# Dense expert gates: GpSimd scatter-adds into a cleared DRAM table instead of one-hot products on TensorE

## The chip, the cores and the metric

The kernel runs on one core of one Trainium2 chip. The metric is the device time of that core in microseconds, the median of several runs. All stages of two transformer blocks are one program, and one launch.

## The reference, cut to what matters

The kernel computes two blocks for 512 tokens of width 1024. The change lies in the last part of the first block, a layer of 16384 experts (128 x 128 keys), of which every token uses 8 x 16 = 128:

```
def peer_ffn(h, w_q, sub_keys, expert_u, expert_v):
    q = (ht @ w_q).reshape(T, 8, 2, 128)
    s = einsum('thpd,hpkd->thpk', q, sub_keys)
    top_s, top_i = top_k(s, 16)                  # per half
    cand = top_s[:, :, 0, :, None] + top_s[:, :, 1, None, :]
    best_s, best_c = top_k(cand.reshape(T, 8, 256), 16)
    expert_idx = ...                             # first key * 128 + second key
    gates = softmax(best_s)
    act = gelu(einsum('td,thkd->thk', x, expert_u[expert_idx]))
    return einsum('thk,thkd->td', gates * act, expert_v[expert_idx])
```

The kernel computes gelu(u_e . x) for all 16384 experts and all 512 tokens. For tokens 0 to 383 it multiplies them with a dense table of gates, which is zero where a token did not choose the expert, and takes the product with v as a dense matmul. The last 128 tokens are treated otherwise: for each of their 128 choices the row of v is fetched and added with its weight.

## The kernel before, in words

**Tiles of weights.** All weights come as a stream of 494 tiles of 128 x 1024 floats (512 KB). SyncE issues `load` (L453) into four slots `w_raw`; a load waits until the tile four places ahead has been split (`split_done`). A tile is split in two fp32r parts, hi (a rounded copy) and lo (the rest). TensorE makes 24 matmuls of 128 x 512 from it (L691 to L693: hi x hi, hi x lo, lo x hi, for eight column blocks). GpSimd's `split` (L558 and L560) makes hi and lo into two buffers `w_hi`, `w_lo`; it waits for the load and for the matmuls of the tile two places back.

**The first layer of experts** (tiles of u) is 128 tiles, one per first key. TensorE sums into banks 0 and 1; ScalarE's `key_act` applies gelu (L1653) and writes the 128 x 512 result to the DRAM tensor `acts` (L1655). Ahead of it are the 16 tiles of `peer_q` and the score matmuls (L971), whose results ScalarE copies (L1642). Alongside the first layer, VectorE makes the choices of each block of 128 tokens: `choose_halves`, `choose`, `places`, `pick_keys`, `chosen_gates`.

**The dense gates before the change.** For tokens 0 to 383, keys and gates of a block are transposed on TensorE (`turn`). VectorE's `one_hots` builds, for four tokens at a time, one-hot rows of both keys (L2437, L2439); GpSimd's `gate_batch` (L574) multiplies one of them with the gate; TensorE's `gate_batches` (L991) makes the 128 x 128 gates of a token as a product of one-hots, in two parts of 128 columns each. ScalarE copies one part (L1664), VectorE adds the other into `gate_stage` (L2449), and ScalarE writes 64 tokens at a time, 4 MB, to the DRAM tensor `gates` (L1676). `LOT_TILES` says how many tiles of u stand between two steps of eight tokens: there are 48 steps of 8 matmuls.

**The second layer of experts** (tiles of v) is 128 tiles in 64 units of two keys. SyncE's `load_unit` loads `acts_in` (L500), `gates_in` (L501) and the two tiles (L508). VectorE multiplies acts with gates (L2507), ScalarE and VectorE split the product (L1696, L2514) and the tiles (L1691, L2520), TensorE makes 24 matmuls of 128 x 384 from a tile. Meanwhile GpSimd fetches, with indirect DMAs, the rows of v (L607, from the DRAM copy `values`, which SyncE's `copy_values` L473 makes during early tiles) and the activations (L615) of the last block of tokens; VectorE's `add_row` adds them (L2528, L2532, L2535). `sums_of_unit` says which rows are added in which unit.

**Order.** Every engine follows its own list of instructions, and semaphores tie the lists. GpSimd issues the first four row fetches and then waits until all of `acts` is written; only then it fetches activations. SyncE's list for the second layer begins after the last `load` of the first layer and after `gates_out`.

Of the kernel before, what the change touches and what calls it, by code (L numbers as in the profile page):

```python
# [15 lines left out]
F32 = mybir.dt.float32  # L16
# [6 lines left out]
P = 128  # L23
# [16 lines left out]
LEAD_TILES, TURN_AT = 12, 10  # L40
LONG, TURNING = (2, 2, 2, 1, 2, 2, 2, 2), (2, 2, 2, 1, 2, 2, 1, 2)
LOT_TILES = (LONG, TURNING, LONG, TURNING, LONG, LONG)
TOKENS_PER_BATCH = 4
HOTS = 2
STAGED_TOKENS = 64
LOTS = P // STAGED_TOKENS
LOT_BATCHES = STAGED_TOKENS // TOKENS_PER_BATCH
STEPS = LOT_BATCHES // HOTS
# [3 lines left out]
COPY_FROM = 8  # L52
PAIR_SLOTS = 4
# [95 lines left out]
def build(nc, x, weights, vectors, tables, keys, lru_gates, out):  # L149
# [80 lines left out]
    hot1 = place("hot1", [P, HOTS, TOKENS_PER_BATCH, 2, NKEYS], A0 + 56 * KB, F32R)  # L230
    peer_q = place("peer_q", [P, 16, T], A0 + 64 * KB)
    stage = place("gate_stage", [P, NKEYS, STAGED_TOKENS], A0 + 64 * KB)
# [12 lines left out]
    gates_t = place("gates_t", [P, P], S1 + 7 * KB + 64)  # L245
    hot2 = place("hot2", [P, HOTS, TOKENS_PER_BATCH, NKEYS], S1 + 8 * KB + 64, F32R)
    gate_part = place("gate_part", [P, HOTS, TOKENS_PER_BATCH, NKEYS], S1 + 12 * KB + 64)
# [3 lines left out]
    expert_w = place("expert_w", [P, KEY_SLOTS, DT], A0 + 8 * KB)  # L251
# [4 lines left out]
    v_hi = place("v_hi", [P, 2, 1024], A0 + 40 * KB, F32R)  # L256
    v_lo = place("v_lo", [P, 2, 1024], A0 + 48 * KB, F32R)
    summed = place("token_sums", [P, 1024], A0 + 4 * KB)
    late_slots = [place(f"v_rows{4 + n}", [P, 1024], at * KB) for n, at in enumerate((48, 52, 56, 60))]
    row_slot = [place(f"v_rows{n}", [P, 1024], A0 + at * KB) for n, at in enumerate((16, 20, 56, 60))] + late_slots  # L260
# [45 lines left out]
    gate_sums = [pair[:].rearrange("p b (t part k) -> p (b t) part k", part=2, k=NKEYS) for pair in (df_banks, banks45)]  # L306


    gates = nc.dram_tensor("gates", (DB * LOTS, NKEYS, NKEYS, STAGED_TOKENS), F32, kind="Internal").ap()
# [3 lines left out]
    def sem(name):  # L313
# [18 lines left out]
    gates_out, out_done = (sem(n) for n in ("gates_out", "out_done"))  # L332

    hi_split, split_done, hot_gated = (sem(n) for n in (
        "hi_split", "split_done", "hot_gated"))
# [110 lines left out]
    def _(sp):  # L446
# [2506 lines left out]
```

## Time and profile before

| | |
|---|---|
| median of 3 runs | 2932.75 us (2931.68 to 2933.92) |
| the profiled execution | 2932.43 us |
| its span | 2930.6 us |
| granted TensorE clock, mean | 0.993 of full |
| TensorE busy | 2870.9 us (98%) |
| GpSimd busy | 2006.7 us (68%) |
| VectorE busy | 1801.6 us (61%) |
| ScalarE busy | 812.7 us (28%) |

A time is read from the start of the span. A matmul's duration in a row overlaps the next one's; what a matmul costs is the distance of two starts. "[x <-E name]" behind a row of the timeline is how long the engine had been idle before it, and what ended that. An engine with a q behind its name (SPq) is that engine's issuing of DMAs. "us to landing" is from the issue of a DMA to its completion.

### The profile page before, as it was taken

Reading aid. Unit: us, or ns where it says so; the run is one execution under the profiler, and the core shown is the slowest. Engines: PE = TensorE matmul, PEld = TensorE weight load, DVE = VectorE, ACT = ScalarE, POOL = GpSimd, SP = SyncE. Lnnn points to the kernel's source line nnn. Section 1 sums busy time; section 2 is a strip of 40 time slices with the busy share of each in tenths; the row PEclk is TensorE's granted clock in tenths of the full one; section 3 lists DMA queues with packets and bytes.
Section 4 is the critical chain, followed back from the end, with each engine's and each line's share of the span. In section 5 each row is a group of like instructions: output and inputs, shape, how many; then the busy total and the mean of one; then the engine's idle time right before and its main releaser. Section 6 shows DMA issues by size and latency. Waiting matters only on the chain.

```text
span 2930.6 us, 39887 instructions
## 1 busy us (share of the span) xinstructions
PE 2870.9 (98%) x13614; PEld 2415.1 (82%) x13614; DVE 1801.6 (61%) x2935; ACT 812.7 (28%) x1351; POOL 2006.7 (68%) x1095
## 2 busy tenths in 40 slices
PE   7999999999999999999999999999999998999998
PEld 6788877788888888888888879999999765778886
DVE  5578664322125678898884028888887767776611
ACT  3244323321011212212221123333333455322201
POOL 6843574477777688999988776565652651678876
PEclk9999999999999999999999999999999998999999
DMA  4533453355664345545555479999996210223322
GB/s 162 185 117 101 142 167 115 115 190 197 216 201 158 101 138 189 187 151 171 188 191 191 146 241 387 361 352 344 358 357 222 86 62 16 76 88 98 95 93 72
DMA packets 269838, 514.79 MB, mean 176 GB/s; under 512 B 120992, under 2 KB 137504, under 8 KB 268704
## 3 DMA queue, kind: packets, MB, share of 16 engines
q1 hardware_dynamic: 226608, 382.02, 40.0%
q0 software_dynamic: 22528, 67.19, 5.9%
q10 hardware_dynamic: 20592, 64.23, 5.7%
q8 instruction: 54, 0.88, 0.1%
q14 instruction: 56, 0.46, 0.0%
HBM read 452.55 MB, written 127.93 MB: 198 GB/s over the span
## 4 chain that ended last, share of the span: by engine, by line
PE 91%; DVE 4%; POOL 1%; issue 1%; ACT 1%; DMA 1%; POOLq 0%; SPq 0%; ACTq 0%; DVEq 0%
PE bank L691 21%; PE bank L693 20%; PE bank L692 20%; PE banks L691 5%; PE banks L692 5%; PE banks L693 5%; PE banks L842 2%; PE banks L991 2%; PE banks L804 1%; PE banks L806 1%; PE banks L805 1%; PE banks L907 1%; PE bank L868 1%; PE banks L898 1%; POOL w_lo L560 1%
## 5 line engine op out<-in xcount | busy, mean ns | idle before, releaser
L558 POOL TENSOR_TENSOR w_hi<-w_raw,ones 128x1024 fp32r<-128x1024 f32 x364 | 696.9, 1915 | 673.1 <-PE bank L693 438.0
L560 POOL TENSOR_TENSOR w_lo<-w_raw,w_hi 128x1024 fp32r<-128x1024 f32 x364 | 893.6, 2455 | 28.6
L691 PE MATMUL bank<-h_hi,w_hi 128*128 128x512 f32 x2000 | 792.5, 396 | 8.1 <-DVE h_lo L2003 7.0
L693 PE MATMUL bank<-h_hi,w_lo 128*128 128x512 f32 x2000 | 780.1, 390 | 0.0
L692 PE MATMUL bank<-h_lo,w_hi 128*128 128x512 f32 x2000 | 779.2, 390 | 0.0
L691 PEld LDWEIGHTS bank<-h_hi,w_hi 128*128 128x128 f32 x2000 | 376.1, 188 | 92.1 <-DVE h_lo L2003 13.9
L693 PEld LDWEIGHTS bank<-h_hi,w_lo 128*128 128x128 f32 x2000 | 375.6, 188 | 79.9
L692 PEld LDWEIGHTS bank<-h_lo,w_hi 128*128 128x128 f32 x2000 | 376.2, 188 | 74.8 <-issue 2.2
L607 POOL DMA_INDIRECT v_rows<-values,v_row_of_choice x128 | 150.1, 1173 | 147.1 <-DVE token_sums L2535 116.6
L1653 ACT ACTIVATE act_out_stage<-bank 128x512 f32<-128x512 f32 x128 | 76.6, 598 | 578.4 <-PE bank L693 511.7
L615 POOL DMA_INDIRECT row_acts<-acts,act_of_choice x128 | 151.5, 1183 | 46.5 <-issue 38.7
L2535 DVE SCALAR_TENSOR_TENSOR token_sums<-v_rows,row_weights,token_sums 128x1024 f32<-128x1024 f32 x127 | 162.8, 1282 | 0.5
L2507 DVE TENSOR_TENSOR expert_w<-acts_in,gates_in 128x384 f32<-128x384 f32 x128 | 68.8, 578 | 142.8 <-DMA gates_in<-gates 142.8
L2437 DVE TENSOR_TENSOR hot<-bank,tab 128x512 fp32r<-128x512 f32 x192 | 123.3, 684 | 50.5 <-PE banks L991 49.8
L1696 ACT ACTIVATE ew_hi<-expert_w 128x384 fp32r<-128x384 f32 x128 | 60.2, 516 | 192.5 <-PE bank L693 183.8
L2514 DVE TENSOR_TENSOR ew_lo<-expert_w,ew_hi 128x384 fp32r<-128x384 f32 x128 | 67.2, 564 | 72.7 <-ACT ew_hi L1696 72.2
L2449 DVE TENSOR_TENSOR gate_stage<-banks,gate_part 128x512 f32<-128x512 f32 x96 | 97.2, 1093 | 17.9 <-DMA gates<-gate_stage 16.1
L574 POOL TENSOR_TENSOR hot<-hot,gates_t 128x512 fp32r<-128x512 f32 x96 | 98.0, 1041 | 5.8 <-DVE hot L2439 2.0
L691 PE MATMUL bank<-ew_hi,v_hi 128*128 128x384 f32 x256 | 86.3, 337 | 6.8 <-DVE ew_lo L2514 6.7
L693 PE MATMUL bank<-ew_hi,w_lo 128*128 128x384 f32 x256 | 86.8, 339 | 0.0
L692 PE MATMUL banks<-ew_lo,w_hi 128*128 128x384 f32 x256 | 86.7, 339 | 0.0
L691 PE MATMUL bank<-ew_hi,w_hi 128*128 128x384 f32 x256 | 86.7, 339 | 0.0
(480 smaller groups left out, 5581.7 us busy)
## 6 DMA issues: line engine op xcount, KB each, us to landing
w_raw<-weights SPq DMA_DIRECT2D x430, 512.0 KB, 3.6
values<-weights SPq DMA_DIRECT2D x128, 512.0 KB, 4.8
acts<-act_out_stage ACTq DMA_DIRECT2D x128, 256.0 KB, 2.9
v_raw<-weights SPq DMA_DIRECT2D x64, 512.0 KB, 6.5
gates<-gate_stage ACTq DMA_DIRECT2D x6, 4096.0 KB, 13.0
acts_in<-acts SPq DMA_DIRECT2D x128, 192.0 KB
gates_in<-gates SPq DMA_DIRECT2D x128, 192.0 KB
resid<-x SPq DMA_DIRECT2D x4, 512.0 KB, 7.7
```

Of the source, the lines that this page charges most:

```text
L558: nc.gpsimd.tensor_tensor(w_hi[:, pair, :], w_raw[:, slot, :], one_col.to_broadcast((P, 1024)), ALU.mult).then_inc(hi_split, 1)
L560: nc.gpsimd.tensor_tensor(w_lo[:, pair, :], w_raw[:, slot, :], f32(w_hi[:, pair, :]), ALU.subtract).then_inc(split_done, 1)
L574: nc.gpsimd.tensor_tensor(hot1[:, p, :, 0, :], f32(hot1[:, p, :, 0, :]), gate.unsqueeze(2).to_broadcast((P, TOKENS_PER_BATCH, NKEYS)), ALU ...
L607: pool.indirect_dma_start(out=row_slot[j % ROW_SLOTS][:], out_offset=None, in_=value_rows, in_offset=bass.IndirectOffsetOnAxis(ap=v_row[:, ...
L615: pool.indirect_dma_start(out=row_act[:, j:j + 1], out_offset=None, in_=act_words, in_offset=bass.IndirectOffsetOnAxis(ap=act_row[:, j:j + ...
L691: mm(out_, hi, rhs_hi, start=first, stop=False)
L692: mm(out_, hi, rhs_lo, start=False, stop=False)
L693: return mm(out_, lo, rhs_hi, start=False, stop=last)
L1653: fn(act_out_s[:, p, :], bank[p][:], ACT.Gelu_apprx_tanh).then_inc(acc_read_act, 1)
L2437: tt_(hot, tokens[key], t_("iota128").unsqueeze(1).to_broadcast(big), ALU.is_equal).then_inc(hot_ready, 1)
L2449: tt_(stage[:, :, first:first + TOKENS_PER_BATCH].rearrange("p k t -> p t k"), gate_sums[p][:, :, 1, :], gate_part[:, p], ALU.add).then_in ...
L2535: stt(summed[:], rows[:], row_w[:, j:j + 1], summed[:], ALU.mult, ALU.add).then_inc(row_summed, 1)
```

## The change

One-hots, turns, the products, the staging and the 4 MB writes are gone. `gates` is now a table of keys x keys x 384 tokens (25 MB). SyncE writes zeros into it with eight DMAs, one behind each of the last eight loads of `peer_q`. When the choices of a block are ready, VectorE computes for each choice its place in the table, and GpSimd adds each gate there with an indirect DMA that accumulates: 128 DMAs of 128 single words per block, three blocks, with a wait after every 16 (a head's choices are distinct, those of two heads need not be). GpSimd no longer splits the tiles of u: ScalarE makes hi (`tile_hi`), VectorE lo (`tile_lo`), with two more buffers (`v_hi`, `v_lo`, which the second layer has), so that four split tiles are held instead of two. `gates_in` is loaded as 1536 contiguous bytes per partition; before it was six runs of 256 bytes. The row sums of the last block begin at unit 5 instead of unit 2, and end one unit later.

```diff
+FIRST_SUMS = 5
 def sums_of_unit(u):
-    return range(max(u - 2, 0) * CHOICES // (UNITS - 4), min(max(u - 1, 0) * CHOICES // (UNITS - 4), CHOICES))
+    n = UNITS - 1 - FIRST_SUMS
+    return range(max(u - FIRST_SUMS, 0) * CHOICES // n, min(max(u + 1 - FIRST_SUMS, 0) * CHOICES // n, CHOICES))
...
             load(tile, n % RAW)
             if COPY_FROM <= n < COPY_FROM + NKEYS:
                 copy_values()
+            clear = n - (len(early) - CLEARS)
+            if clear == 0:
+                sp.wait_ge(consts_set, 3)
+            if clear >= 0:
+                some = NKEYS // CLEARS
+                sp.dma_start(gates[clear * some:clear * some + some, :, :].rearrange("e k t -> k e t"),
+                             zeros[:].unsqueeze(1).to_broadcast((P, some, DT))).then_inc(gates_cleared, 16)
...
-                sp.dma_start(g_in[:, slot, :].rearrange("p (b t) -> p b t", t=STAGED_TOKENS),
-                             gates[:, :, bass.ds(key, 1), :].rearrange("b k a t -> k b (a t)")).then_inc(key_in[u], 16)
+                sp.dma_start(g_in[:, slot, :], gates[bass.ds(key, 1), :, :].rearrange("a k t -> (a k) t")).then_inc(key_in[u], 16)
...
-        sp.wait_ge(gates_out, c.due(gates_out, 16 * DB * LOTS))
+        for n in range(DB):
+            sp.wait_ge(gates_added[n], 16 * CHOICES)
...
+        def add_gates(n):
+            pool.wait_ge(rows_ready, n + 1)
+            for j in range(CHOICES):
+                if j and j % HEAD_CHOICES == 0:
+                    pool.wait_ge(gates_added[n], 16 * j)
+                pool.indirect_dma_start(
+                    out=gate_words, out_offset=bass.IndirectOffsetOnAxis(ap=gate_at[:, n, j:j + 1], axis=0),
+                    in_=gate_of[:, n, j:j + 1], in_offset=None, compute_op=ALU.add).then_inc(gates_added[n], 16)
+        pool.wait_ge(gates_cleared, 16 * CLEARS)
+        for n in range(DB):
+            add_gates(n)
...
+        def tile_hi(n):
+            at = START["experts"] + n
+            act.wait_ge(raw_loaded[n % RAW], 16 * (at // RAW + 1))
+            act.wait_ge(tile_done, at - RAW + 1)
+            fn(value_slot(n)[0], w_raw[:, n % RAW, :], ACT.Copy).then_inc(v_hi_ready, 1)
...
+        for key in range(NKEYS - 2):
+            if key + 3 < NKEYS:
+                tile_hi(key + 3)
+            key_act(key, key % 2)
+            if key % CHOICE_TILES == SHARES_AT and key // CHOICE_TILES < TT:
+                shares()
...
+        def tile_lo(n):
+            hi, lo = value_slot(n)
+            dve.wait_ge(v_hi_ready, n + 1)
+            tt_(lo, w_raw[:, n % RAW, :], f32(hi), ALU.subtract).then_inc(split_done, 1)
...
+        for n in range(2, NKEYS):
+            tile_lo(n)
+            if n - 2 < TT * CHOICE_TILES:
+                choices((n - 2) // CHOICE_TILES, (n - 2) % CHOICE_TILES)
```

`choices(tt, part)` spreads the choices of a block over 14 tiles of u (`CHOICE_TILES`); its last part, 13, computes the places (`place_rows`). `zeros` is a 128 x 384 buffer set once by VectorE.

SyncE's list at the last loads of `peer_q`, in the kernel before (`w_raw` loads are the weights, `values` the DRAM copies):

```order
L453 DMA w_raw<-weights 128x1024 [waits split_done]
L473 DMA values<-weights 128x2x512
L453 DMA w_raw<-weights 128x1024 [waits split_done]
L473 DMA values<-weights 128x2x512
L453 DMA w_raw<-weights 128x1024 [waits split_done] x8
```

and the same place in the changed kernel:

```order
L449 DMA w_raw<-weights 128x1024 [waits split_done]
L469 DMA values<-weights 128x2x512
L488 DMA gates<-zeros 128x16x384
L449 DMA w_raw<-weights 128x1024 [waits split_done]
L488 DMA gates<-zeros 128x16x384
L449 DMA w_raw<-weights 128x1024 [waits split_done]
L488 DMA gates<-zeros 128x16x384
L449 DMA w_raw<-weights 128x1024 [waits split_done]
L488 DMA gates<-zeros 128x16x384
L449 DMA w_raw<-weights 128x1024 [waits split_done]
L488 DMA gates<-zeros 128x16x384
L449 DMA w_raw<-weights 128x1024 [waits split_done] x4
```

Each clear of 16 x 128 x 384 floats now stands in the queue between a load and the next one; the first four clears have a copy of values before them too.

GpSimd's list in the first layer, before (`hot_100` is a one-hot buffer):

```order
L558 TENSOR_TENSOR w_hi<-w_raw,ones 128x1024 [waits tile_done,raw_loaded2,split_done]
L560 TENSOR_TENSOR w_lo<-w_raw,w_hi 128x1024 [waits hi_split]
L558 TENSOR_TENSOR w_hi<-w_raw,ones 128x1024 [waits tile_done,raw_loaded3,split_done]
L560 TENSOR_TENSOR w_lo<-w_raw,w_hi 128x1024 [waits hi_split]
L574 TENSOR_TENSOR hot_100<-hot_100,gates_t 128x4x128 [waits hot_ready,split_done]
L574 TENSOR_TENSOR hot_100<-hot_100,gates_t 128x4x128 [waits hot_ready]
```

and in the changed kernel, from the end of block 0 of the gates to the start of block 1:

```order
L580 DMA gates<-gate_of_choice,gate_row_of_choice 6291456x1 [waits gates_added0]
L580 DMA gates<-gate_of_choice,gate_row_of_choice 6291456x1 x15
L580 DMA gates<-gate_of_choice,gate_row_of_choice 6291456x1 [waits rows_ready]
L580 DMA gates<-gate_of_choice,gate_row_of_choice 6291456x1 x15
L580 DMA gates<-gate_of_choice,gate_row_of_choice 6291456x1 [waits gates_added1]
```

Splits and products are gone from GpSimd there. A block is 8 x 16 scatters with 7 waits for the scatters before; between blocks there is only the wait for the choices.

VectorE's list where the row sums begin, before (`ew_lo` and `v_lo` are what TensorE's next unit waits for):

```order
L2520 TENSOR_TENSOR v_lo<-v_raw,v_hi 128x1024 [waits v_hi_ready]
L2528 TENSOR_TENSOR row_weights<-row_acts,chosen 128x8 [waits row_act_in0]
L2532 TENSOR_SCALAR token_sums<-v_rows_130,row_weights 128x1024 [waits v_row_in0,rows_ready]
L2514 TENSOR_TENSOR ew_lo<-expert_w,ew_hi 128x384 [waits ew_hi_ready,weighted] x2
L2520 TENSOR_TENSOR v_lo<-v_raw,v_hi 128x1024 [waits v_hi_ready]
```

and the same place in the changed kernel:

```order
L2422 TENSOR_TENSOR v_lo<-v_raw,v_hi 128x1024 [waits v_hi_ready]
L2416 TENSOR_TENSOR ew_lo<-expert_w,ew_hi 128x384 [waits ew_hi_ready,weighted] x2
L2422 TENSOR_TENSOR v_lo<-v_raw,v_hi 128x1024 [waits v_hi_ready]
```

The wait for `row_act_in0` has moved from unit 2 to unit 5, three units on.

## Rows read from the trace of the kernel before

**Rows 1.** Stretches: length, busy PE, PEld, DVE, ACT, POOL; PE clock, DMA share, GB/s.
```profile
1752.00:1764.00 12.00, 5.35 (x22) 5.03 (x21) 6.43 (x10) 2.38 (x4) 9.39 (x9) 0.72 1.08 394
1800.00:2200.00 400.00, 400.00 (x2292) 400.00 (x2291) 334.67 (x401) 140.75 (x191) 238.75 (x203) 1.00 1.02 357
```

**Rows 2.** Timeline of PE: start, us, instruction. First layer's start and end.
```profile
989.21 0.48 PE L691 MATMUL bank<-h_hi,w_hi 128*128 128x512 f32 x1
...
1735.93 0.45 PE L691 MATMUL bank<-ew_hi,v_hi 128*128 128x384 f32 x1 [0.16 <-ACT act_out_stage L1653]
```

**Rows 3.** Timeline of PE: two steps of one-hot products, two tiles apart.
```profile
1055.12 1.11 PE L991 MATMUL banks<-hot,hot 128*128 128x256 f32 x8
...
1066.98 1.11 PE L991 MATMUL banks<-hot,hot 128*128 128x256 f32 x8
```

**Rows 4.** Timeline of POOL: two splits of tiles, with no gate work between.
```profile
1588.53 1.89 POOL L558 TENSOR_TENSOR w_hi<-w_raw,ones 128x1024 fp32r<-128x1024 f32 x1 [1.07 <-PE bank L693]
...
1593.97 1.89 POOL L558 TENSOR_TENSOR w_hi<-w_raw,ones 128x1024 fp32r<-128x1024 f32 x1 [1.08 <-PE bank L693]
```

**Rows 5.** Timeline of DVE and of PE, where the row sums begin.
```profile
1757.53 0.17 DVE L2528 TENSOR_TENSOR row_weights<-row_acts,chosen 128x8 f32<-128x8 f32 x1 [8.98 <-DMA row_acts<-acts,act_of_choice]
...
1759.11 0.69 PE L691 MATMUL bank<-ew_hi,v_hi 128*128 128x384 f32 x1 [6.65 <-DVE ew_lo L2514]
1759.59 0.52 PE L692 MATMUL bank<-ew_lo,v_hi 128*128 128x384 f32 x1
1759.91 0.52 PE L693 MATMUL bank<-ew_hi,v_lo 128*128 128x384 f32 x1
```

**Rows 6.** Timeline of SP and of POOL, at the last tiles of peer_q.
```profile
906.53 0.34 SPq L453 DMA_DIRECT2D w_raw<-weights  x1
...
963.33 1.89 POOL L558 TENSOR_TENSOR w_hi<-w_raw,ones 128x1024 fp32r<-128x1024 f32 x1 [1.08 <-PE bank L693]
```

**Rows 7.** DMA queues in 1590 to 1690 us, packets, MB, share of 16 engines.
```profile
q1 hardware_dynamic: 2736, 9.96, 33.2%
q10 hardware_dynamic: 2780, 5.04, 13.1%
...
w_raw<-weights SPq DMA_DIRECT2D x18, 512.0 KB, 3.6
```

**Rows 8.** The same queue view, in 800 to 900 us.
```profile
q1 hardware_dynamic: 7488, 18.88, 56.2%
```

**Rows 9.** DMAs issued in 1139 to 1141 us, behind one another on one queue.
```profile
gates<-gate_stage ACTq DMA_DIRECT2D x1, 4096.0 KB, 13.2
acts<-act_out_stage ACTq DMA_DIRECT2D x1, 256.0 KB, 13.6
```

**Rows 10.** GpSimd's indirect DMAs: durations min/median/max, idle before, landing of row fetches (L607).
```profile
L615 POOL DMA_INDIRECT row_acts<-acts,act_of_choice x128: 940/952/1949, 1742.8 to 2205.9; - x128
...
L615 POOL DMA_INDIRECT row_acts<-acts,act_of_choice x128 | 151.5, 1183 | 46.5 <-issue 38.7
...
DMA to landing us min/median/max: 4.4/7.6/10.3
```

**Rows 11.** Landing of ScalarE's 256 KB writes to DRAM (L1655).
```profile
DMA to landing us min/median/max: 2.0/2.9/13.8
```

**Rows 12.** Timeline of ACT and of DVE: hi and lo; start and end of one block's choices.
```profile
1736.36 1.06 ACT L1691 ACTIVATE w_hi<-w_raw 128x1024 fp32r<-128x1024 f32 x1 [0.48 <-ACT act_out_stage L1653]
...
1737.45 1.23 DVE L2520 TENSOR_TENSOR w_lo<-w_raw,w_hi 128x1024 fp32r<-128x1024 f32 x1 [4.46 <-ACT w_hi L1691]
...
980.94 3.19 DVE L2307 MAX8 top_s<-scores 128x8 f32<-128x128 f32 x16 [50.65 <-ACT scores L1642]
...
1038.01 0.29 DVE L2407 TENSOR_TENSOR chosen<-chosen 128x128 f32<-128x128 f32 x1
```

**Rows 13.** Timeline of SP and of DVE: the first load for the second layer, and its use.
```profile
1708.21 0.34 SPq L500 DMA_DIRECT2D acts_in<-acts  x1
...
1714.55 4.08 DVE L2507 TENSOR_TENSOR expert_w<-acts_in,gates_in 128x384 f32<-128x384 f32 x2 [139.77 <-DMA gates_in<-gates]
```

More of the change, by code:

```diff
@@ L305, in build @@
     bank += [nc.alloc_psum_tensor(f"bank{n}", [P, T], F32) for n in range(6, 8)]
[L306 to L309 removed]
+    gates = nc.dram_tensor("gates", (NKEYS, NKEYS, DT), F32, kind="Internal").ap()
     values = nc.dram_tensor("values", (NKEYS, P, 2, 512), F32, kind="Internal").ap()
@@ L666, in _ @@
         c.repeat((N_STREAM - START["up"]) // RAW, four)
-        splits((N_STREAM - START["up"]) % RAW)
+        for s in range((N_STREAM - START["up"]) % RAW):
+            split(s)
         for j in range(0, KT, 2):
@@ L995, in _ @@
-        tiles_fm(TURN_AT, h_hi, h_lo, acc_read_act)
-        pe.wait_ge(score_read, c.due(score_read, 0))
-        turn(0)
-        tiles_fm(LEAD_TILES - TURN_AT, h_hi, h_lo, acc_read_act)
-        def mixed(n, first, next_choices=0):
-            gate_batches()
-            for k in range(n):
-                p = (first + k) % 2
-                pe.wait_ge(acc_read_act, c.due(acc_read_act, 1, back=2))
-                tile_fm(p, h_hi, h_lo, bank[p][:])
-                if k == 0 and next_choices:
-                    turn(next_choices)
@@ L1007, in twos @@
-        def twos(n, first):
-            c.repeat(n, lambda i: mixed(2, first))
-        tile = LEAD_TILES
-        for lot in range(DB * LOTS):
-            first = tile % 2
-            twos(3, first)
-            mixed(1, first)
-            if LOT_TILES[lot] == TURNING:
-                twos(2, 1 - first)
-                mixed(1, 1 - first, (lot + 1) // LOTS)
-                mixed(2, first)
-            else:
-                twos(4, 1 - first)
-            tile += sum(LOT_TILES[lot])
-        tiles_fm(NKEYS - tile, h_hi, h_lo, acc_read_act)
@@ L1022, in _, with first_layer @@
-        pe.wait_ge(gate_read, c.due(gate_read, 0))
+        def first_layer(i):
+            for n in range(RAW):
+                hi, lo = value_slot(n)
+                pe.wait_ge(acc_read_act, c.due(acc_read_act, 1, back=2))
+                pe.wait_ge(split_done, c.due(split_done))
+                for k in range(KT):
+                    col = slice(k * P, (k + 1) * P)
+                    ins = three(bank[n % 2][:], hi[:, col], lo[:, col], h_hi[:, k, :], h_lo[:, k, :], k == 0, k == KT - 1)
+                ins.then_inc(tile_done, 1)
@@ L1638, in _ @@
         evac(8, peer_q, first=8)
+        def tile_hi(n):
[3 more added lines that the diff above has]
+            fn(value_slot(n)[0], w_raw[:, n % RAW, :], ACT.Copy).then_inc(v_hi_ready, 1)
+        for n in range(2):
+            tile_hi(n)
         for tt in range(TT):
@@ L2498, in _, with choices @@
-        gates_summed(DB * per_block - 1)
+            ve.tensor_copy(gate_at[:, tt, :] if tt < DB else act_row[:], low_f[:]).then_inc(rows_ready, 1)
+        def tile_lo(n):
+            hi, lo = value_slot(n)
+            dve.wait_ge(v_hi_ready, n + 1)
+            tt_(lo, w_raw[:, n % RAW, :], f32(hi), ALU.subtract).then_inc(split_done, 1)
+        def choices(tt, part):
+            if part in (0, 1, 3, 4):
+                choose_halves(tt, *{0: (0, 5), 1: (5, 9), 3: (9, 14), 4: (14, 16)}[part])
+            elif part == 5:
+                choose(0, PEER_HEADS // 2)
+            elif part == 6:
+                choose(PEER_HEADS // 2)
+            elif part == 8:
+                places(tt)
+            elif part == 9:
+                pick_keys(tt, 0)
+            elif part == 10:
+                picked(0)
+                pick_keys(tt, 1)
+            elif part == 12:
+                picked(1)
+                chosen_gates(tt)
+            elif part == 13:
+                place_rows(tt)
```

234 lines of the change are left out of this document (50 added, 184 removed).

## The prediction

> **What bounds the kernel now.** I read the busy times first, then the windows of the expert layers, then TensorE's own waits. In a steady stretch of the second layer TensorE is busy 400 of 400 us at full clock [rows 1]; the first layer is as dense. So an engine's saving counts only where it takes matmuls off TensorE's list or ends a wait of TensorE, and the three other engines matter by when they deliver.
>
> The first layer starts at 989.21 and the second at 1735.93 [rows 2]: 746.7 us for 128 tiles. With no gate work between, a tile takes 1593.97 - 1588.53 = 5.44 us [rows 4]. 128 x 5.44 = 696.3, so the gate work holds TensorE for 50.4 us. Almost all is the 48 steps of products: two steps are 11.86 us apart with two tiles between [rows 3], 11.86 - 10.88 = 0.98 us each, 47 us; the rest is the three turns.
>
> The largest wait inside the expert layers is where the row sums begin. VectorE sits 8.98 us in front of the first `row_weights`, because the activations are not fetched yet; `ew_lo` of unit 2 stands behind it, and TensorE waits 6.65 us [rows 5]. Its clock falls with that: the next matmuls start 0.32 us apart [rows 5], against 400/2292 = 0.175 us in the steady stretch [rows 1], some ten of them (the clock is 0.72 in that window), so 1.5 us more.
>
> **What the change does, part by part.** The sum is made against the profiled execution's own 2932.43 us, 0.3 us under the median.
>
> 1. *Products, turns and their waits go.* -50.4 us, all of it on TensorE's list. ScalarE's copies, VectorE's one-hots and sums and the 4 MB writes were beside it: nothing for them.
>
> 2. *Sums begin at unit 5.* A unit is 48 x 0.175 = 8.4 us, so the wait stands 25 us later, and the missing 8.98 us are long over. GpSimd's order there is the same. -6.65 - 1.5 = -8.2 us. The sums end a unit later, with 128/58 = 2.2 rows in a unit for 2.13: VectorE was busy 334.67 of 400 [rows 1], and 0.07 rows more do not fill it.
>
> 3. *The tiles of u are split by ScalarE and VectorE.* hi costs 1.06 us and lo 1.23 us [rows 12], per tile of 5.44. ScalarE has room. VectorE is the tight one: the choices of a block took 980.94 to 1038.30 = 57.4 us by themselves [rows 12]; now they lie over 14 tiles, 76.2 us, together with 14 x 1.23 = 17.2 us of lo and some 2 us of places, 77 us in all. Part of the 57.4 was waiting for GpSimd's splits, which are gone. And hi of a tile is made as soon as the tile four places back is done, three tiles or 16.3 us before it is needed; less 2.3 for hi and lo, VectorE may be 14 us behind before TensorE notices. 0 us; the bound is 4 blocks x 1 to 4 us (rival D).
>
> 4. *The clears.* Eight writes of 25.17/8 = 3.146 MB go on SyncE's queue, each in front of the next tile. Does a load wait for them? On ScalarE's queue a 256 KB write issued behind a 4 MB write landed after 13.6 us, the 4 MB after 13.2 [rows 9], where such a write alone lands in 2.9 [rows 11]. A queue keeps its order, so yes. What a clear takes is not in the trace; writes to DRAM in 2 KB runs took 13.1% of 100 us for 5.04 MB [rows 7], 385 GB/s, so 8.2 us for a clear in 1.5 KB runs. That is my value, as the nearest row in kind and size. The slow end is the loads' own 9.96 MB in 33.2 us [rows 7], 300 GB/s, 10.5 us; the fast end is that the load passes the clears, no cost at all. The Trainium skill, "DMA: Bandwidth & Descriptors", Specifications, gives about 358 GB/s as a core's limit to HBM; by that a clear would be 8.8 us as an estimate, and the sum 4 us higher; the 385 GB/s of this trace are above it, so I stay with the row.
>
>    A load takes 0.524 MB/300 = 1.75 us of the queue, a copy of `values` (3.1 us for load and copy at 18.88 MB in 56.2 us [rows 8]) another 1.4; four of the clears have one. The load of tile 8 of `peer_q` goes out at 906.53 [rows 6]; the load of tile 15 is behind 7 clears, 7 loads and 4 copies: 906.5 + 57.4 + 12.3 + 5.6 + 3.6 (landing [rows 7]) = 985.4. GpSimd began to split that tile at 963.33, after 1.08 us of idleness [rows 6]. It is 22.1 us late, less 1.1: +21.0 us on TensorE, spread over the last four or five tiles. The load after the eighth clear, first of the first layer, has the 15 us of score matmuls in front of its use and adds nothing. After such gaps the clock falls, as above: +1.6. Together +22.6 us; at 300 GB/s 16 us more.
>
> 5. *The scatters.* GpSimd issues 384, and SyncE's first load for the second layer waits for all. No row shows an accumulating DMA. The nearest is the gather of single words: 0.94 us at its best, 1.95 at its worst, and 38.7/127 = 0.30 between two [rows 10]. In the second layer the mean was 1.18 [rows 10], with VectorE busy 334.67 of 400 us [rows 1], mostly with operations on two SBUF inputs; in the first layer those are lo, 1.23 of 5.44 us, and a few of the choices, so I take 1.0 + 0.3 = 1.3 us. For a landing I take 4.4, the fastest row fetch; the ends are 2.0 (fastest write to DRAM [rows 11]) and 7.6 [rows 10]. A block is 121 issues and 7 waits: 121 x 1.3 + 7 x 4.4 = 188 us. Block 0 can begin when VectorE has its places, behind lo of tile 15: the layer starts at 989.2 + 22.6 = 1011.8, tile 11 ends at 1077, places at 1083. Three blocks end at 1083 + 3 x 188 = 1647. Needed: the second layer starts at 1011.8 + 696.3 = 1708.1, and from the load of acts to its use in VectorE were 6.3 us [rows 13] and some 2 to `ew_lo`: 1700. There are 53 us to spare; 0 us. The ends of the price: 121 x 1.24 + 7 x 2.0 = 164, and 121 x 1.48 + 7 x 7.6 = 232 us, which ends at 1779, 79 us late. The cover is GpSimd's freedom from splits; blocks 1 and 2 never wait for choices.
>
> 6. *gates_in in long runs* lightens the DMA queues of the second layer (share 1.02 [rows 1]). TensorE did not wait for them in 1800 to 2200: 0.
>
> Sum: 2932.4 - 50.4 - 8.2 + 22.6 = **2896.4 us**, 1.2% less.
>
> **The rivals.**
> *A: the scatters come late, and the kernel gets slower.* Mechanism: GpSimd cannot issue at 1.3 us, or the waits after each head are long, and TensorE stands before the second layer until `gates_added` is full. For it: the same instruction varied from 0.94 to 1.95 us beside VectorE, the accumulation is unpriced, and it is a serial chain of 617 us to fit. Against: the median is 0.952. It costs nothing up to 617/3 = 205.7 us a block; the gain of 36 us is gone from 653/3 = 217.7, that is from 1.5 us per issue with a landing of 5.2 us. At 232 a block: 2896.4 + 79 = 2975 us. If an issue or its transfer cost 2.2 us, 297 a block, it would be 3170. The Trainium skill, "SBUF — State Buffer", in its note on DVE blocking software DMA, says that GpSimd cannot write descriptors while VectorE holds the port they share; in this trace that agrees with the slow ones of rows 10, and it speaks against this change.
> *B: the clears cost nothing*, because a load passes them or they drain faster than the row says. For it: four tiles of slack. Against: rows 9. 2932.4 - 58.6 = 2873.8 us.
> *C: the clears cost more*, 300 GB/s or a queue that SyncE stands in front of: 2896.4 + 16 = 2912, up to 2925 with a landing of scatters just too late. Short runs of 1.5 KB speak for it.
> *D: VectorE runs short* in the first 57 tiles: 4 blocks x 1 to 4 us, 2900 to 2912. It is a case of C's size and counted there.
>
> **How the numbers follow.** Forecast (2885 to 2907) 0.46; B (2870 to 2885) 0.20; C and D (2907 to 2926) 0.14; A 0.20, of it 0.02 just at the old time and 0.18 above. What a measurement of this kernel can tell from no change is about 0.2%, 6 us. Faster: 0.46 + 0.20 + 0.12 = 0.78; same 0.04; slower 0.18. The range reaches from B's end to A at a block of 223 us, 2950; it leaves out 0.04 below (B with a gain I have not seen) and 0.14 of A above: 2868 to 2950.
>
> **What would show it.** Right: no one-hot matmul; a first layer of 696 us; idle gaps of 4 to 5 us of TensorE in front of `peer_q` tiles 12 to 15, each ended by GpSimd's split, itself ended by the load, 20 us in all; the last scatter near 1650 us; no 6.65 us wait in unit 2. Wrong: gaps in the first layer ended by `w_lo` or `v_lo` of VectorE; TensorE idle before the second layer, ended by `gates_in`; scatters over 1.5 us apart; or no gaps at the clears. In the first of these VectorE's choices are at fault, in the next two the scatters, in the last the order of the queue.

## The result, and the profile after

The changed kernel takes 3083.15 us (median of 4 runs, 3078.72 to 3084.21) where the kernel before takes 2932.66 (4 runs): a ratio of 1.051, interval 1.050 to 1.053. It is 150 us slower. The prediction was 2896.4 us with a range up to 2950: wrong in size and in sign. What happened is rival A, at a price for a scatter (1.96 us) above the bound of 1.48 us in the sum. Of the runs of the kernel before that were taken beside the experiments, one of 4175.65 us at a mean granted clock of 0.643 is left out of every comparison.

The profiled execution took 3084.21 us, its span 3082.4. From its page, the busy times, the chain that ended last, and the group of matmuls with the long wait:

```profile
span 3082.4 us, 38555 instructions
...
PE 2837.4 (92%) x13218; PEld 2372.3 (77%) x13218; DVE 1644.4 (53%) x2683; ACT 896.4 (29%) x1383; POOL 1975.1 (64%) x1127
...
POOL gates L580 19%; PE bank L679 12%; PE bank L681 11%; PE bank L680 11%; PE banks L679 5%; PE banks L680 5%; PE banks L681 5%; DMA gates<-gate_of_choice,gate_row_of_choice 3%; DMA w_raw<-weights 2%; PE banks L830 2%; PE banks L792 1%; PE banks L794 1%; PE banks L793 1%; PE banks L895 1%; POOL w_hi L561 1%
...
L679 PE MATMUL bank<-ew_hi,v_hi 128*128 128x384 f32 x256 | 86.5, 338 | 178.8 <-DVE v_lo L2422 178.8
```

TensorE does 33.5 us less work than before (2870.9) and is idle for 185 us more. The third line is the chain that ended last: 19% of the span are GpSimd's scatters (L580), which were to lie beside TensorE's work. The last line holds a wait of 178.8 us. TensorE's waits (us in total, times, longest) show that it is one single wait:

```profile
PE bank L679 <- DVE v_lo L2422: 178.8, 1, 178.8
PE bank L679 <- POOL w_lo L563: 13.4, 9, 4.6
```

Its timeline across the border of the two layers, and at the start of the first layer, answers to [rows 2]:

```profile
1008.27 0.48 PE L679 MATMUL bank<-h_hi,v_hi 128*128 128x512 f32 x1
...
1713.63 0.39 PE L681 MATMUL bank<-h_hi,w_lo 128*128 128x512 f32 x1
1892.82 0.66 PE L679 MATMUL bank<-ew_hi,v_hi 128*128 128x384 f32 x1 [178.80 <-DVE v_lo L2422]
1893.27 0.53 PE L680 MATMUL bank<-ew_lo,v_hi 128*128 128x384 f32 x1
1893.59 0.53 PE L681 MATMUL bank<-ew_hi,v_lo 128*128 128x384 f32 x1
```

The releaser named is `v_lo`, but that is only the last link. VectorE's list has the first products of acts and gates ahead of `v_lo`, and those wait for the gates. All instructions that touch `gates` (durations min/median/max in ns, first and last start; then what GpSimd's queue was idle for in front of them, and who waited for them):

```profile
L580 POOL DMA_INDIRECT gates<-gate_of_choice,gate_row_of_choice x384: 1545/1548/2600, 1080.5 to 1870.7; - x192
...
  issue: 129.4, 362
  DVE gate_row_of_choice L2364: 94.8, 1
  DMA gates<-gate_of_choice,gate_row_of_choice: 48.2, 21
...
  DVE expert_w L2409: 188.3, 1
```

Read this as a book of the chain. 384 scatters start between 1080.5 and 1870.7: 790 us, 263 a block, where 188 were predicted. A scatter holds GpSimd for 1.55 us (the median; the mean is 1.60, 614.2 us for 384) and the next one starts 129.4/362 = 0.36 us later: 1.96 us each in the mean, 1.85 in the regular case. The 21 waits for a head to land cost 48.2/21 = 2.3 us. The end follows link by link: last scatter 1870.7, first load for the second layer 1873.8, first product on VectorE 1883.7, first matmul 1892.8.

The stretches (columns as in [rows 1]), with the steady one last, show the hole, the slow start behind it (granted clock 0.93 in 40 us; the first matmuls start 0.32 us apart) and that nothing is left of it 40 us later:

```profile
1713.00:1893.00 180.00, 1.20 (x6) 0.73 (x5) 4.65 (x8) 5.02 (x8) 127.66 (x84) 0.51 0.29 39
1893.00:1933.00 40.00, 40.00 (x216) 40.00 (x217) 23.21 (x33) 13.53 (x19) 21.81 (x20) 0.93 0.98 375
1933.00:2333.00 400.00, 400.00 (x2292) 400.00 (x2291) 337.07 (x404) 141.41 (x192) 245.87 (x205) 1.00 0.95 356
```

At the clears, GpSimd's split of the last four tiles of `peer_q` answers to [rows 6]; the last of them starts at 981.38 where it started at 963.33:

```profile
954.11 1.89 POOL L561 TENSOR_TENSOR w_hi<-w_raw,ones 128x1024 fp32r<-128x1024 f32 x1 [5.99 <-DMA w_raw<-weights]
963.21 1.90 POOL L561 TENSOR_TENSOR w_hi<-w_raw,ones 128x1024 fp32r<-128x1024 f32 x1 [4.79 <-issue]
972.24 1.90 POOL L561 TENSOR_TENSOR w_hi<-w_raw,ones 128x1024 fp32r<-128x1024 f32 x1 [4.69 <-DMA w_raw<-weights]
981.38 1.90 POOL L561 TENSOR_TENSOR w_hi<-w_raw,ones 128x1024 fp32r<-128x1024 f32 x1 [4.83 <-issue]
```

**The book of the spans.** -50.4 for products and turns and -8.2 for the sums, both as forecast, +19.1 for the clears (first layer at 1008.27 for 989.21), +9.3 because the first layer takes 705.6 us instead of 696.3, +178.8 for the wait, +2.7 for the slow start behind it: +151.3. Measured: 3082.4 - 2930.6 = 151.8. One reading in it is off: in the kernel before, the second layer starts at 1735.08 and not at 1735.93 (that row is its fourth matmul), so the gate work held TensorE for 49.6 us and not 50.4, and the sum is +152.1.

### The profile page after: what moved, and what is told of

It is laid out like the page before. It is cut to its first block, busy times and chain, and to the rows that moved or that the text cites. A ratio compares the mean times of both kernels' runs of the same rounds, so it can differ in the third digit from the quotient of the medians.

```text
span 3082.4 us, 38555 instructions
## 1 busy us (share of the span) xinstructions
PE 2837.4 (92%) x13218; PEld 2372.3 (77%) x13218; DVE 1644.4 (53%) x2683; ACT 896.4 (29%) x1383; POOL 1975.1 (64%) x1127
## 4 chain that ended last, share of the span: by engine, by line
PE 62%; POOL 20%; DVE 6%; issue 6%; DMA 4%; ACT 1%; SPq 0%; POOLq 0%; ACTq 0%; DVEq 0%
POOL gates L580 19%; PE bank L679 12%; PE bank L681 11%; PE bank L680 11%; PE banks L679 5%; PE banks L680 5%; PE banks L681 5%; DMA gates<-gate_of_choice,gate_row_of_choice 3%; DMA w_raw<-weights 2%; PE banks L830 2%; PE banks L792 1%; PE banks L794 1%; PE banks L793 1%; PE banks L895 1%; POOL w_hi L561 1%
## 5 line engine op out<-in xcount | busy, mean ns | idle before, releaser
L561 POOL TENSOR_TENSOR w_hi<-w_raw,ones 128x1024 fp32r<-128x1024 f32 x236 | 454.2, 1925 | 584.3 <-PE bank L681 335.3
L580 POOL DMA_INDIRECT gates<-gate_of_choice,gate_row_of_choice x384 | 614.2, 1599 | 272.3 <-issue 129.4
L679 PE MATMUL bank<-h_hi,w_hi 128*128 128x512 f32 x1488 | 594.4, 399 | 20.5 <-POOL w_lo L563 13.4
L563 POOL TENSOR_TENSOR w_lo<-w_raw,w_hi 128x1024 fp32r<-128x1024 f32 x236 | 585.4, 2480 | 18.5
L681 PE MATMUL bank<-h_hi,w_lo 128*128 128x512 f32 x1488 | 582.1, 391 | 0.0
L680 PE MATMUL bank<-h_lo,w_hi 128*128 128x512 f32 x1488 | 581.3, 391 | 0.0
L679 PEld LDWEIGHTS bank<-h_hi,w_hi 128*128 128x128 f32 x1488 | 280.9, 189 | 88.8 <-POOL w_lo L563 17.2
L679 PE MATMUL bank<-ew_hi,v_hi 128*128 128x384 f32 x256 | 86.5, 338 | 178.8 <-DVE v_lo L2422 178.8
L679 PE MATMUL bank<-h_hi,v_hi 128*128 128x512 f32 x512 | 202.3, 395 | 0.0
L681 PE MATMUL bank<-h_hi,v_lo 128*128 128x512 f32 x512 | 201.9, 394 | 0.0
L680 PE MATMUL bank<-h_lo,v_hi 128*128 128x512 f32 x512 | 201.9, 394 | 0.0
```

The costliest lines, as they stand in the source:

```text
L561: nc.gpsimd.tensor_tensor(w_hi[:, pair, :], w_raw[:, slot, :], one_col.to_broadcast((P, 1024)), ALU.mult).then_inc(hi_split, 1)
L563: nc.gpsimd.tensor_tensor(w_lo[:, pair, :], w_raw[:, slot, :], f32(w_hi[:, pair, :]), ALU.subtract).then_inc(split_done, 1)
L580: pool.indirect_dma_start(out=gate_words, out_offset=bass.IndirectOffsetOnAxis(ap=gate_at[:, n, j:j + 1], axis=0), in_=gate_of[:, n, j:j + ...
L679: mm(out_, hi, rhs_hi, start=first, stop=False)
L680: mm(out_, hi, rhs_lo, start=False, stop=False)
L681: return mm(out_, lo, rhs_hi, start=False, stop=last)
```

## The experiments

Each ratio is to the kernel before in the same batch of runs. Its median was 2932.5 us in the batch of experiments 7 and 8, as beside the result, and 2944 to 2945 us in the others; one chip gave both. The traces differ in the same way, and in one place. From its first matmul to its last, the second layer takes 546.1 us in the kernel before, 539.7 in the changed one, and 538.7 and 539.1 in experiments 7 and 8. In the traces of the other experiments it takes 542.2 to 568.4 us, mostly for stops of TensorE in its first 50 us that the profile names issue, which is to say that it shows no wait. Experiments 2, 6, 9 and 10 have these stops though their edits have little in common, and the kernel before, of which no trace was taken there, is 12 us slower in these batches too. So I put them down to the batch and not to an edit; their cause is not known. Times are therefore compared within a batch, by ratio or by difference.

**1. Plain scatters.** What is the price of the accumulation?

```diff
-                    in_=gate_of[:, n, j:j + 1], in_offset=None, compute_op=ALU.add).then_inc(gates_added[n], 16)
+                    in_=gate_of[:, n, j:j + 1], in_offset=None).then_inc(gates_added[n], 16)
```

> The changed kernel, with scatters that write the gates instead of adding them (so a choice that two heads of a token share keeps one gate only). Theory: it is the accumulation that makes a scatter cost 1.55 us of GpSimd plus 0.30 between two; a plain one costs what the gathers do, 0.95 + 0.30. Then the last scatter is issued near 1080 + 3 x (121 x 1.25 + 7 x 3.9) = 1080 + 536 = 1616 us, TensorE does not wait before the second layer, and the time is 3083 - 178.8 - 2.7 (slow clock after the wait) = 2901 us. Rival: it is the direction, writing single words to DRAM; then issue and time stay, 3083 us.

Measured: 3302.45 us (one run), ratio 1.122, where the changed kernel has 1.051. The price of an issue came out as expected, the time did not. The scatters, and two stretches of 100 us, in the second of which they are over (columns as in [rows 1]):

```profile
L580 POOL DMA_INDIRECT gates<-gate_of_choice,gate_row_of_choice x384: 952/958/1832, 1078.3 to 1651.5; - x192
```

```profile
1100.00:1200.00 100.00, 36.89 (x75) 20.98 (x74) 19.21 (x88) 4.96 (x6) 72.64 (x74) 0.57 0.10 29
1700.00:1800.00 100.00, 100.00 (x437) 81.86 (x436) 22.06 (x18) 30.44 (x37) 3.34 (x4) 1.00 0.48 166
```

A plain scatter takes 0.96 us, like the gathers of [rows 10] at their median; accumulating adds 0.59 us of GpSimd's time. But from some 20 us after the first scatter TensorE stops between instructions, with no semaphore that ends it (issue), 290 us in all. ScalarE and VectorE slow down too; what ends ScalarE's stops is mostly named remote, a release whose sender the profile does not have. From the timeline:

```profile
1122.38 0.59 PE L679 MATMUL bank<-h_hi,v_hi 128*128 128x512 f32 x1 [1.51 <-issue]
...
1136.51 0.60 ACT L1617 ACTIVATE act_out_stage<-bank 128x512 f32<-128x512 f32 x1 [24.67 <-remote]
```

TensorE is busy 37 of 100 us there, and the DMA engines 10% of the time. While the scatters last (1080 to 1651 us) it makes 832 matmuls; in the changed kernel it makes 2489 in the same stretch. Experiment 6 comes back to this.

**2. Half of the choices.** Does the chain of scatters hold the second layer up, and nothing else? The loop goes to `CHOICES // 2`, and SyncE waits for as many.

> The changed kernel with only the first 64 choices of a block added to the table (the gates of four heads are left out). Theory: the chain of scatters is all that makes it slower. 192 scatters end near 1080 + 396 = 1476 us, long before the first layer's end, the wait of 178.8 us vanishes with the 2.7 us of slow clock behind it: 2901 to 2902 us, which is what the rest of the change gives. Rival: other waits of the second layer, DMA traffic or VectorE's lag stand behind the scatters: over 2910 us.

Measured: 2911.54 us (2907.91 to 2918.02), ratio 0.989 (0.987 to 0.992). The scatters end at 1477.8:

```profile
L580 POOL DMA_INDIRECT gates<-gate_of_choice,gate_row_of_choice x192: 1547/1548/2599, 1081.6 to 1477.8; - x192
```

No wait of TensorE is left in front of the second layer; the largest inside the expert layers is that of the clears:

```profile
PE bank L679 <- POOL w_lo L563: 13.2, 9, 3.3
```

By its absolute time this would be the rival, which said over 2910 us. But the kernel before took 2944.2 us beside it, and 0.9892 of the 2932.66 us of the result is 2901, as the theory has it. So the other parts of the change together do give a gain, 32.7 us, near the 36 that I had forecast for the whole, and the chain turns it into a loss.

**3. The sums back to unit 2**, on top of 2.

```diff
-    n = UNITS - 1 - FIRST_SUMS
-    return range(max(u - FIRST_SUMS, 0) * CHOICES // n, min(max(u + 1 - FIRST_SUMS, 0) * CHOICES // n, CHOICES))
+    return range(max(u - 2, 0) * CHOICES // (UNITS - 4), min(max(u - 1, 0) * CHOICES // (UNITS - 4), CHOICES))
```

> As e2_half, and the row sums begin at unit 2 again, as in the kernel before. Theory: the wait of VectorE for the activations comes back, with TensorE's 6.65 us and 1.5 us of slow clock: 8 us over e2_half. Rival: with the lighter loads of gates_in the activations come in time, and the two are equal.

Measured: 2916.94 us (2912.62 to 2923.29), 5.4 us above experiment 2 as medians, with ranges that overlap; 8 were expected. The wait of [rows 5] is back among TensorE's waits:

```profile
PE bank L678 <- DVE ew_lo L2415: 5.8, 1, 5.8
```

**4. 16 clears of half the size**, on top of 2 (`CLEARS = 16`).

> As e2_half, with the table cleared in 16 parts behind the last 16 loads instead of 8 behind 8. Theory: a load waits for the clears before it on SyncE's queue; in the changed kernel a load with its clear takes 9.0 us of the queue and with a copy of values 10.2, so a clear 7.2. Half a clear makes 6.6 us with a copy, 5.4 without, against 5.44 us of a tile: 12 x 1.1 = 13 us of backlog, about the slack of four tiles, so TensorE's waits there shrink from 19 us to 0 to 3: 16 to 19 us under e2_half. Rival: the bytes cost the same wherever they are: no difference.

Measured: 2893.38 us (2891.69 to 2898.54), ratio 0.984 (0.981 to 0.987), 18.2 us under experiment 2. Of the 13.2 us of waits for `w_lo` this is left:

```profile
PE bank L679 <- POOL w_lo L563: 1.1, 4, 0.3
```

That is also what the kernel before has without clears (1.1 us in 4 waits). The same bytes, begun eight tiles earlier, fit into the slack of the queue.

**5. The sums alone, in the kernel before** (the edit of `sums_of_unit`, and nothing else of the change).

> The kernel before with the change of the row sums alone: 128 sums over units 5 to 62, the gates still by one-hot products. Theory of the prediction (its second term, and the half-scatter pair, where sums from unit 2 cost 5.4 us): TensorE's wait of 6.65 us for VectorE in unit 2 goes with the matmuls at half clock behind it, and the first wait for the row loads shrinks, so 5 to 8 us less than before, about 2925 to 2928 us where before has 2933, and no wait for ew_lo over 1 us in the chain. Rival: the sums packed into 58 units instead of 60 leave VectorE short somewhere else in the second layer, and the time is that of before within 2 us.

Measured: 2937.27 us (12 runs, 2927.34 to 2948.10) where the kernel before had 2944.4 (16 runs, 2932.54 to 2946.67), ratio 0.9976 (0.9962 to 0.9991). Single runs of the two overlap; it is the medians that differ, by 7 us, as expected. TensorE's wait for `ew_lo` is gone. The term holds, and this one edit is already a little faster than both kernels.

**6. Experiment 1 again, and with spaced scatters.** Was it an accident; and if not, is it the kind of the scatters or their rate?

```diff
                     in_=gate_of[:, n, j:j + 1], in_offset=None).then_inc(gates_added[n], 16)
+                nc.gpsimd.memset(zeros[:], 0.0).then_inc(paced, 1)
+                pool.wait_ge(paced, n * CHOICES + j + 1)
```

> The first experiment once more, timed: if the slow stretches belong to the kernel, its time is again 250 to 400 us above the time of the kernel before, with gaps named issue of over 100 us on TensorE in the first layer; if they were an accident of one execution, it is about 2890 to 2930 us (scatters that end by about 1650 us hide behind the first layer).

> Plain scatters as in the first experiment (no sum in the table, so its contents are not the gates), with a small memset on GpSimd behind each, so that they start further apart than 1.26 us. In the first experiment every engine went slowly while the plain scatters ran, without a wait that the profile names. Theory of the rate: it was their pitch, and at a pitch near the 1.85 us of the accumulating ones TensorE has no such gaps in the first layer; its time is then near that of the changed kernel for its own last scatter (384 times the pitch behind 1080 us). Theory of the kind: single-word writes without a sum hold the other engines up at any pitch, and the gaps named issue stay above 100 us in total.

Measured: experiment 1 again takes 3346.94 us (2 runs), ratio 1.137 (1.134 to 1.140), so it was no accident. With the memset 3069.13 us (one run), ratio 1.042: the starts are 1.68 us apart instead of 1.26 and the scatters end at 1836.4. TensorE is now busy throughout the first layer,

```profile
1100.00:1300.00 200.00, 200.00 (x873) 163.75 (x872) 175.27 (x619) 69.19 (x82) 156.85 (x199) 1.00 0.45 144
```

and its loss is one wait in front of the second:

```profile
PE bank L682 <- DVE v_lo L2425: 141.0, 1, 141.0
```

TensorE's stops named issue sum to under 10 us in the whole kernel. So it is how closely the plain scatters follow one another, not their kind. Why one every 1.26 us stops TensorE is not shown; that its supply of instructions is starved is a guess that no run tested.

**7. Half of the words.** What does GpSimd pay for? Each scatter is cut to 64 partitions (`gate_at[0:64, ...]`, `gate_of[0:64, ...]`).

> The changed kernel, with each scatter cut to the first 64 of its 128 words (half of the tokens of a block get no gates). In the changed kernel an issue takes 1.55 us whatever VectorE does. If GpSimd pays by the word, an issue takes some 0.8 to 1.0 us, the scatters end before 1600 us, and the time is that of half the choices, about 2900 to 2915 us; if it pays by the DMA, an issue stays at 1.5 us or more and the time at about 3080 us.

Measured: 3034.96 us (one run), ratio 1.035. It lies between the two theories, nearer to the second: an issue takes 1.41 us for 1.55, and the last scatter starts 48 us earlier.

```profile
L580 POOL DMA_INDIRECT gates<-gate_of_choice,gate_row_of_choice x384: 1405/1411/2434, 1080.5 to 1822.3; - x192
```

64 words more cost 0.137 us, 2.1 ns a word. If that holds down to no words, an estimate from two sizes, some 1.27 of the 1.55 us belong to the DMA and not to its words. The chain is long mainly because it has 384 links, not because it moves 49152 words.

**8. Heads of two blocks in turn, and 16 clears**, all scatters kept. Tokens of two blocks never meet at an address, so GpSimd need not wait for a head to land while it issues one of the other block.

```diff
+        half = PEER_HEADS // 2
+        heads = [(0, h) for h in range(half)]
+        for n in range(DB - 1):
+            for h in range(half):
+                heads += [(n, half + h), (n + 1, h)]
+        heads += [(DB - 1, half + h) for h in range(half)]
+        for n, h in heads:
+            add_head(n, h)
```

> The changed kernel with all its scatters, 16 clears instead of 8, and heads of two blocks in turn on GpSimd, so that a wait for the landing is left at 9 places of 21. By the book of the chain (384 x 1.94 us of issue and distance, 2.3 us for each wait): first scatter at 1061, last at 1061 + 744 + 21 = 1826 us for 1871, the wait of TensorE in front of the second layer 27 us shorter and the clears 18 us cheaper: about 45 us less than the changed kernel, ratio to the kernel before about 1.035. Rival: the DMA engines, not GpSimd, set the pace, and then the landings grow by what the waits save, and only the 18 us of the clears are gained, ratio 1.045.

Measured: 3025.17 us (3023.36 to 3026.12), ratio 1.031 (1.030 to 1.033): 58 us under the changed kernel, where 45 were expected. Scatters from 1062.9 to 1813.7, with 22.7 us of waiting in 9 waits, 2.5 us each: the landings hardly grew (2.3 before), so GpSimd's own issuing is the pace. Even so TensorE waits 138.9 us in front of the second layer, for 178.8: 40 us of the 58 are the shorter chain, the rest the clears. 384 issues do not fit.

**9. The place of the weights.** In the first layer of the changed kernel a matmul from `v_hi`, `v_lo` starts 0.2324 us after the one before it (mean in 1500 to 1700 us), one from `w_hi`, `w_lo` 0.2268 (over 420 of each). In the second layer it is the other way round, in both kernels: 0.1734 and 0.1759 (over 550 of each). `w` lies at 16 to 32 KB of a partition, `v` at 135 to 151 KB; the moving operand is `h`, at 32 to 64 KB, in the first layer, and `ew`, at 159 to 175 KB, in the second. In the kernel of experiment 5 I moved `v` to where `h_lo` was (and four of the eight buffers of row fetches, which lay there, to the old place of `v`):

```diff
-    v_hi = place("v_hi", [P, 2, 1024], A0 + 40 * KB, F32R)
-    v_lo = place("v_lo", [P, 2, 1024], A0 + 48 * KB, F32R)
+    v_hi = place("v_hi", [P, 2, 1024], 48 * KB, F32R)
+    v_lo = place("v_lo", [P, 2, 1024], 56 * KB, F32R)
...
-            act.wait_ge(tile_done, VALUES + n - RAW + 1)
+            act.wait_ge(tile_done, VALUES + max(n - RAW + 1, 0))
```

> The kernel before with sums from unit 5, and in the second layer the pair of weight slots v_hi, v_lo moved from the upper part of the SBUF partition (136 KB and up, roughly) to 48 and 56 KB, where h lay; ScalarE's first two tiles of values wait for the last tile of the first layer. Theory of place: the start-to-start time of matmuls depends on whether the weights lie in the same part of the partition as the moving operand; here the moving operand (ew_hi, ew_lo) is in the upper part, so the v pair goes from 0.1734 us to the 0.1758 us of the w pair. Theory of the slot (who writes it, or when): the v pair stays at 0.1734 us. The late start costs some 3 us in all either way.

Measured: in the second layer matmuls from `v` now start 0.1761 us apart, those from `w` 0.1760 (over 540 of each, stops left out). So it is the address of the weights and not who writes them or when. What about the address it is stays open: the upper buffers all start 128 bytes past a whole KB and the lower ones on a whole KB, so the move changed the offset as well as the part, and the first layer had no such test. The time, 2962.32 us (one run), is 25 us over experiment 5. TensorE waits 5.9 us for the first `v_lo`, the slower pace of 64 tiles is worth 64 x 24 x 0.0027 = 4 us, and 17 us are stops named issue, like those of experiment 6 from the same batch.

**10. Two blocks by scatters, the third by one-hots.** By experiment 8, the time between the first choices and the second layer holds two blocks of scatters, not three. This kernel scatters blocks 0 and 1 as there, clears only their columns, and makes block 2 with the products of the kernel before, a step of 8 matmuls behind every fourth tile from tile 51 on, all one-hots on VectorE. TensorE's part:

```diff
-        c.repeat(NKEYS // RAW, first_layer)
+        c.repeat(TURN_AFTER // RAW, first_layer)
+        pe.wait_ge(score_read, c.due(score_read, 0))
+        turn()
+        c.repeat(HOT_STEPS, with_gates)
+        c.repeat((NKEYS - TURN_AFTER) // RAW - HOT_STEPS, first_layer)
```

> Blocks 0 and 1 by scatters (256, heads of the two blocks in turn), block 2 by one-hot products as in the kernel before (16 steps of 8 matmuls; VectorE makes all of the one-hots), 16 clears of two thirds of the table, sums from unit 5. By the book: the kernel with half of the words of choices and 16 clears stood at a ratio of 0.984, and the products of one block put back 16 x 0.98 us and a turn, some 17 us: ratio 0.990, about 2903 us where before has 2932.7. The scatters end at 1062 + 256 x 1.94 + 9 x 2.3 = 1580 us, and TensorE has no wait over 1 us in front of the second layer. Rival: VectorE, which now makes choices, lo and one-hots at once around tiles 48 to 58, or the 4 MB of stage that is written in runs of 256 bytes, holds TensorE up, 5 to 20 us, ratio 0.992 to 0.997.

Measured: 2931.15 us (6 runs) for 2944.96 of the kernel before, ratio 0.9952 (0.9940 to 0.9964), where 0.990 was expected. By ratio it is the fastest version that computes everything, though its interval just overlaps that of experiment 5, the one edit of the sums (0.9962 to 0.9991). The scatters end in time, at 1599:

```profile
L598 POOL DMA_INDIRECT gates<-gate_of_choice,gate_row_of_choice x256: 1546/1547/2568, 1061.2 to 1599.3; - x128
```

9.0 us of TensorE's waits are for ScalarE's results:

```profile
PE bank L704 <- ACT act_out_stage L1666: 9.0, 3, 5.2
```

The timeline shows where the two long ones come from. ScalarE issues a 4 MB write of the stage, in runs of 256 bytes, and then stands for 12 us in the issue of the next write on the same queue:

```profile
1641.18 0.52 ACTq L1684 DMA_DIRECT2D gates<-gate_stage  x1
...
1646.24 12.22 ACTq L1668 DMA_DIRECT2D acts<-act_out_stage  x1
...
1660.24 0.79 PE L704 MATMUL bank<-h_hi,v_hi 128*128 128x512 f32 x1 [3.63 <-ACT act_out_stage L1666]
```

The first 4 MB write, at 1454.44, does the same: 13.68 us in the issue, and TensorE waits 5.19. That is the second half of the rival: 8.8 of the 9.0 us. In the kernel before six writes of 4 MB, each partition's part in one piece, held ScalarE up at none of the issues behind them (0.34 us each). The second layer takes 562.0 us here for 546.1 in the trace of the kernel before, but that trace is of another batch: beside this experiment the kernel before took 12 us more. So the ratio falls short of the forecast by 15 us, of which 9 are explained.

## Why the prediction was wrong, point by point

1. *Products and turns, -50.4.* They went, but the 64 tiles that now come from `v_hi` and `v_lo` cost 24 x 0.0056 = 0.134 us more each, 8.6 of the 9.3 us by which the first layer is longer than forecast. 5.44 us a tile was read where all weights came from `w`; the change put half of them elsewhere, and I counted buffers, not addresses. Of the 50.4 us, 0.8 were the misread start of the second layer.

2. *Sums from unit 5, -8.2.* Right in mechanism; in size 5.4 us (experiment 3) and 7.1 us (experiment 5), both differences of medians whose runs overlap.

3. *Splitting by ScalarE and VectorE, 0.* Right. TensorE has no gap in the first layer at all, though VectorE is busy 190.60 of 220 us at its densest (rows under rival A). Rival D fell.

4. *The clears, +22.6.* Near, at +19.1, but partly by luck, since two errors offset each other: five waits for `w_lo` sum to 12.3 us where I had 21.0, and the granted clock of 0.88 in 936 to 990 us costs some 6 us where I had 1.6. The loads do queue behind the clears (rival B fell), and more than that, SyncE stands in their issue, as rival C had it, at no more than the price of the sum:

```profile
946.24 8.43 SPq L449 DMA_DIRECT2D w_raw<-weights  x1
```

From 954.11 to 981.38 are three tiles, 9.09 us for a load and a clear of 3.67 MB in all, 404 GB/s; I had allowed 1.75 + 8.2 = 9.95. The Trainium skill's 358 GB/s ("DMA: Bandwidth & Descriptors", Specifications) as a core's limit to HBM lies under these 404, and would have moved the sum further the wrong way.

5. *The scatters, 0.* **This is the step that failed**: the price of a scatter, and with it the overlap of the chain with the first layer, put at 0 us and measured at 178.8. The start was right (1083 predicted, 1080.5). The price was not: "so I take 1.0 + 0.3 = 1.3 us" from one issue to the next, measured 1.85 in the regular case and 1.96 in the mean. The landing erred a little the other way: 1.60 + 2.3 = 3.9 us from issue to the next head, for 4.4. By my own formula, 121 x 1.96 + 7 x 3.9 = 264 a block, which ends at 1080.5 + 793 = 1874, where I had 1647. My outer bound, 1.48 us, was the slowest mean of an operation that does not accumulate; that is no bound for one that does. The text said "the accumulation is unpriced" and then priced it at nothing. From last scatter to first matmul passed 22.1 us, of which I had allowed 12.7 (4.4, 6.3 and 2).

6. *gates_in in long runs, 0.* Right: TensorE is busy 400 of 400 us, share 0.95 for 1.02.

*Rival A* named the wait, its place and the point of decision, 1.5 us per issue. Of its reasons the unpriced accumulation was the right one (experiment 1), and the one it led with was not: that VectorE holds GpSimd's issues back. The Trainium skill's note on DVE blocking software DMA ("SBUF — State Buffer"), which stood beside it, speaks of VectorE's two-port modes; no row here shows in which mode an operation ran. As the main price this trace speaks against it: the same scatters from 1080 and from 1500 us on (ns), and VectorE's load in such stretches, 191 of 220 us and 44 of 213 (columns as in [rows 1]):

```profile
L580 POOL DMA_INDIRECT gates<-gate_of_choice,gate_row_of_choice x103: 1547/1548/2542, 1080.5 to 1298.5; - x103
...
L580 POOL DMA_INDIRECT gates<-gate_of_choice,gate_row_of_choice x184: 1545/1547/2589, 1499.1 to 1868.8; - x184
```

```profile
1080.00:1300.00 220.00, 220.00 (x960) 180.15 (x959) 190.60 (x694) 74.72 (x89) 171.39 (x103) 1.00 0.62 143
1500.00:1713.00 213.00, 213.00 (x930) 174.46 (x929) 44.13 (x36) 60.33 (x73) 164.89 (x105) 1.00 0.58 126
```

The median does not move. The mean does by 171.39/103 - 164.89/105 = 0.09 us: so much VectorE's load may be worth, against 0.59 for the accumulation. VectorE is in the tail: issues of up to 2.6 us occur beside its instructions, while the 191 scatters that meet none of them take at most 1.72. The chance of 0.20 for A was too small, since a chain of 384 with 53 us of slack in 617 stood on a price that no row showed.

## What to carry to other kernels

Before work is moved onto a serial chain of small indirect DMAs, multiply: issues times the price of exactly this form of issue, against the time until the first reader needs the result. With hundreds of links, 0.1 us of price is 38 us of time, and a neighbour's price (a gather for a scatter that accumulates) is no bound. Cut links (fewer choices by this way, the rest by another) before cutting words, and let two independent chains take turns, so that one's landing hides behind the other's issues. Ask also what a large write in short runs does to the engine that issues the next DMA on its queue: here it stood there for 8 to 14 us.

## What the runs showed of the hardware that I had not expected

- GpSimd's indirect DMA of 128 single words: 0.96 us of issue if it writes, 1.55 if it accumulates, 1.41 if it accumulates 64 words; 0.30 us between two.
- With plain scatters every 1.26 us TensorE made a third of its matmuls (832 for 2489 in 571 us; ratio 1.137 for the whole kernel); every 1.68 us it stayed busy. The cause is open.
- An engine can stand in the issue of a DMA behind a large write on its queue: 8.4 us behind a clear of 3.1 MB in runs of 1.5 KB, 12.2 and 13.7 us behind 4 MB in runs of 256 bytes, 0.34 us behind 4 MB that leave each partition in one piece.
- Matmuls of 512 columns start 0.2268 us apart with weights and moving operand both in the lower part of the partition, 0.2324 with the weights in the upper; of 384 columns 0.1734 with both in the upper part, 0.1761 with the weights in the lower. Whether the part decides or the offset within a KB was not tested.
